# A two-layer decoder trunk on one core: the SwiGLU down projection by seven block products for eight, with its weights' sums and low parts made by GpSimd

## What is computed

```python
def swiglu(x, w_gate, w_up, w_down):
    return (jax.nn.silu(x @ w_gate) * (x @ w_up)) @ w_down
...
    f = swiglu(rms_norm(h, ffn_pre_g[i]), w_ff_gate[i], w_ff_up[i], w_ff_down[i])
    h = h + rms_norm(f, ffn_post_g[i])
    gate = jax.nn.sigmoid(rms_norm(h, ple_norm_g[i]) @ w_ple_gate[i])
    h = h + (p[i] @ w_ple_proj[i]) * gate
```

## Time and profile before

| what | value |
|---|---|
| median of 3 runs | 2053.27 us (2048.46 to 2055.60) |
| the profiled execution's own time | 2056.85 us |
| its span, first to last instruction | 2055.1 us |
| its mean granted TensorE clock | 0.987 of full |
| PE, DVE, ACT, POOL busy | 96%, 65%, 37%, 8% of the span |

### The profile page before, as it was taken

One profiled execution on the slowest core, in us unless ns is written; L12 is line 12 of the kernel. 1 busy time (PEld: TensorE's weight loads), 2 busy tenths in 40 slices (PEclk: granted clock), 3 DMA queues, 4 the chain that ended last, 5 costly groups with the idle time before them and its releaser, 6 DMA issues.

```text
span 2055.1 us, 27329 instructions
## 1 busy us (share of the span) xinstructions
PE 1983.0 (96%) x9412; PEld 1631.3 (79%) x9412; DVE 1330.7 (65%) x2126; ACT 750.5 (37%) x1402; POOL 161.1 (8%) x218
## 2 busy tenths in 40 slices
PE   6789999999999999999999997999999999999999
PEld 6668888888888878888866686788888888888887
DVE  5885666666566667477578657666566666655763
ACT  4552222333222243343268644333222233322431
POOL 2200000000000011110036311000000000000110
PEclk8999999999999999999999998999999999999999
DMA  5232222233232251231000112233232223323402
GB/s 187 99 106 93 89 79 87 77 102 97 82 92 78 86 194 37 67 108 52 0 11 2 52 52 97 82 103 97 82 92 77 86 77 102 97 82 106 170 11 82
DMA packets 214756, 173.25 MB, mean 84 GB/s; under 512 B 8608, under 2 KB 196384, under 8 KB 214688
## 3 DMA queue, kind: packets, MB, share of 16 engines
q1 hardware_dynamic: 212960, 166.08, 25.6%
q10 hardware_dynamic: 1728, 6.29, 0.9%
HBM read 159.75 MB, written 12.58 MB: 84 GB/s over the span
## 4 chain that ended last, share of the span: by engine, by line
PE 89%; DVE 6%; POOL 2%; issue 1%; DMA 1%; ACT 1%; SPq 0%; DVEq 0%; ACTq 0%
PE ps L285 15%; PE ps L287 15%; PE ps L286 15%; PE ps L690 13%; PE ps L692 13%; PE ps L691 13%; POOL probs L1352 1%; PE ps L346 1%; DVE ps L1317 1%; PE ps L1306 1%; PE ps L1360 1%; PE ps L563 1%; DVE t_lo L933 1%; PE ps L467 1%; DMA H<-in_x 0%
## 5 line engine op out<-in xcount | busy, mean ns | idle before, releaser
L1008 DVE TENSOR_TENSOR H<-H,ps 128x512 f32<-128x512 f32 x320 | 218.0, 685 | 142.2 <-PE ps L287 142.2
L285 PE MATMUL ps<-wd_hi,ffn_a_hi 128*128 128x512 f32 x704 | 275.1, 391 | 2.4 <-DVE H L1008 1.8
L287 PE MATMUL ps<-wd_hi,ffn_a_lo 128*128 128x512 f32 x704 | 274.6, 390 | 0.0
L286 PE MATMUL ps<-wd_lo,ffn_a_hi 128*128 128x512 f32 x704 | 274.5, 390 | 0.0
L690 PE MATMUL ps<-t_hi,s_hi 128*128 128x512 f32 x528 | 207.7, 393 | 16.8 <-DVE t_lo L933 16.1
L691 PE MATMUL ps<-t_lo,s_hi 128*128 128x512 f32 x528 | 207.0, 392 | 0.0
L692 PE MATMUL ps<-t_hi,s_lo 128*128 128x512 f32 x528 | 206.9, 392 | 0.0
L776 ACT ACTIVATE s_hi<-s_raw 128x512 fp32r<-128x512 f32 x176 | 111.1, 633 | 228.3 <-DVE s_raw L896 225.0
L896 DVE TENSOR_TENSOR s_raw<-s_raw,a_raw 128x512 f32<-128x512 f32 x88 | 60.8, 691 | 191.1 <-DMA s_raw<-in_w_ff_gate 143.6
L800 ACT ACTIVATE m<-ps 128x512 f32<-128x512 f32 x44 | 25.9, 589 | 405.0 <-PE ps L692 405.0
L285 PEld LDWEIGHTS ps<-wd_hi,ffn_a_hi 128*128 128x128 f32 x704 | 132.6, 188 | 31.4 <-issue 4.0
(11 more groups left out here) (208 smaller groups left out, 4183.3 us busy)
## 6 DMA issues: line engine op xcount, KB each, us to landing
a_raw<-in_w_ff_gate SPq DMA_DIRECT2D x88, 256.0 KB, 2.9
a_raw<-in_w_ff_up SPq DMA_DIRECT2D x88, 256.0 KB, 3.0
s_raw<-in_w_ff_up SPq DMA_DIRECT2D x88, 256.0 KB, 2.9
s_raw<-in_w_ff_gate SPq DMA_DIRECT2D x88, 256.0 KB, 3.0
wd_raw<-in_w_ff_down SPq DMA_DIRECT2D x44, 512.0 KB, 4.2
residual_spill<-H SPq DMA_DIRECT2D x16, 512.0 KB, 2.6
raw<-in_w_ple_gate SPq DMA_DIRECT2D x16, 512.0 KB, 5.7
back<-residual_spill SPq DMA_DIRECT2D x16, 512.0 KB, 6.9
```

What stands on the lines that cost most here:

```text
L285: pe.matmul(out_, lhs[0], rhs[0], start=first, stop=False)
L286: pe.matmul(out_, lhs[0], rhs[1], start=False, stop=False)
L287: return pe.matmul(out_, lhs[1], rhs[0], start=False, stop=last)
L1008: dve.tensor_tensor(dst, dst, ps[:, 4 + n % 4, :], ALU.add).then_inc(F["summed"][n % 4], 1)
```

## The change

The down projection of a group is done by the same scheme of seven for eight. Its tokens are taken in two halves (h = 0, 1) of 512; in each, a block is two token tiles (j = 0, 1) by one channel tile, and the weights' blocks are channel tile by column half. That is 7 blocks by 2 token tiles by 3 matmuls = 42 matmuls a half, 84 a group. A half now needs: four sums of activation blocks (`d_sums`, DVE, 128x256), their high and low parts (`d_his` ACT, `d_los` DVE), four bank copies (ACT) and 12 additions to H (`d_adds`, DVE) where there were 8. The two halves are not run after the group: they stand inside the next group's first tile, h = 0 after S3 and h = 1 after S1. In the layer's last group they stand at the end with nothing beside them.

The sums of weight blocks (gate, up and down) move from DVE to Pool, and so do the low parts of the seven down weight blocks, in four batches (three of 128x1024, one of 128x512). The sigmoid and DVE's product become one Silu on ACT. S2's sum is written into A21's slot; S3's low part lies over S3's raw block, which S2's sum reads, so `form_lo` of S3 now waits for S2's sum. Loads are put in a new order; the region of SBUF grows by 2 KB a partition. Cut to its core (`d_sums`, `d_his` and the copies left out):

```diff
+        DOWN = (("S3", 0, 7), ("A11", 0, 4), ("A11", 1, 3), ("S3", 1, 6), ("A12", 0, 4), ("S2", 0, 5), ("A12", 1, 3),
+                ("S2", 1, 7), ("S1", 0, 5), ("A22", 0, 6), ("S1", 1, 7), ("S4", 0, 5), ("A22", 1, 3), ("S4", 1, 7))
...
+        def ffn_load_down(sp, L, g):
+            sp.wait_ge(F["down"], PRODUCTS * (half_of(L, g, 0) + 1))
...
+        def ffn_load_tile(sp, L, g, t):
+            if not is_first(g, t):
+                ffn_load_after(sp, "S4", "a12", L, g, t, preceding(g, t))
+            if not is_last(g, t):
+                n = following(g, t)
+                ffn_load_after(sp, "A11", "a11", L, *n, (g, t))
+                sp.wait_ge(F["form_sum"], nth_sum("S4", L, g, t))
+                ffn_load(sp, "A21", "a21", L, *n)
+                for name, source in (("S3", "a11"), ("S2", "a22"), ("A12", "a12"), ("S1", "a22")):
+                    ffn_load_after(sp, name, source, L, *n, (g, t))
+            if t == 0 and not is_first(g, t):
+                ffn_load_down(sp, L, g)
+            if not is_last(g, t):
+                ffn_load_after(sp, "A22", "a22", L, *n, (g, t))
...
+        def ffn_pe_tile(pe, L, g, t):
...
             ffn_product(pe, "S3", L, g, t)
+            if t == 0:
+                ffn_pe_down(pe, L, g - 1, 0, (g, t))
...
             ffn_product(pe, "S1", L, g, t)
+            if t == 0:
+                ffn_pe_down(pe, L, g - 1, 1, (g, t))
             ffn_product(pe, "A22", L, g, t)
...
+        def ffn_act_second(act, L, g):
+            t, p, n = 1, (g, 0), following(g, 1)
+            gate_silu(act, L, *p, 1)
+            copy_first(act, L, g, t)
+            form_hi(act, "A22", L, g, t)
+            form_hi(act, "S4", L, g, t)
+            copy_m7(act, L, g, t)
+            wd_his(act, L, g, (0, 1))
+            copy_u(act, L, g, t)
+            wd_his(act, L, g, (2, 3))
+            if not is_last(g, t):
+                form_hi(act, "A11", L, *n)
+            gate_silu(act, L, g, t, 0)
...
+        def wd_los(pool, L, g):
+            r = GROUPS * L + g
+            pool.wait_ge(F["wd_sum"], 4 * r + 4)
+            for b in range(4):
+                slots = slice(2 * b, min(2 * b + 2, 7))
+                pool.wait_ge(F["wd_hi"], 4 * r + b + 1)
+                pool.tensor_tensor(wd_lo[:, slots, :], wd_raw[:, slots, :], wd_hi[:, slots, :].bitcast(F32), ALU.subtract
+                                   ).then_inc(F["wd"], 1)
...
+        def ffn_pool(pool, L, g):
+            n1, n2 = (g, 1), (g + 1, 0)
+            if not is_first(g, 0):
+                form_sum(pool, "S4", L, g, 0)
+            for name in ("S3", "S1", "S2"):
+                form_sum(pool, name, L, *n1)
+            wd_sums(pool, L, g)
+            form_sum(pool, "S4", L, *n1)
+            if not is_last(*n1):
+                form_sum(pool, "S3", L, *n2)
+            wd_los(pool, L, g)
+            if not is_last(*n1):
+                for name in ("S1", "S2"):
+                    form_sum(pool, name, L, *n2)
...
         def form_lo(dve, name, L, g, t):
             dve.wait_ge(F["form_hi"], nth(name, L, g, t))
+            if name == "S3":
+                dve.wait_ge(F["form_sum"], nth_sum("S2", L, g, t))
...
+        def ffn_dve_tile(dve, L, g, first_group=False):
+            t, p, n, down = 0, preceding(g, 0), following(g, 0), g - 1
+            times_up(dve, L, *p, 1)
+            form_lo(dve, "S2", L, g, t)
+            d_los(dve, L, down, 0)
...
+            d_adds(dve, L, down, 0, first_group)
+            form_lo(dve, "A12", L, g, t)
+            d_sums(dve, L, down, 1)
+            form_lo(dve, "S1", L, g, t)
+            d_los(dve, L, down, 1)
+            form_lo(dve, "A22", L, g, t)
+            form_lo(dve, "S4", L, g, t)
+            d_adds(dve, L, down, 1, first_group)
+            up_second_half(dve, L, g, t)
+            form_lo(dve, "A11", L, *n)
+            form_lo(dve, "S3", L, *n)
+            up_first_half(dve, L, g, t)
+            times_up(dve, L, g, t, 0)
+            form_lo(dve, "S2", L, *n)
+
+        def ffn_dve_second(dve, L, g):
+            t, p, n = 1, (g, 0), following(g, 1)
+            times_up(dve, L, *p, 1)
+            for name in ("A12", "S1", "A22", "S4"):
+                form_lo(dve, name, L, g, t)
+            if not is_last(g, t):
+                form_lo(dve, "A11", L, *n)
+            up_second_half(dve, L, g, t)
+            up_first_half(dve, L, g, t)
+            times_up(dve, L, g, t, 0)
+            d_sums(dve, L, g, 0)
+            if not is_last(g, t):
+                form_lo(dve, "S3", L, *n)
...
+                times_up(dve, L, last, 1, 1)
+                d_los(dve, L, last, 0)
+                d_adds(dve, L, last, 0)
+                d_sums(dve, L, last, 1)
+                d_los(dve, L, last, 1)
+                ffn_post(dve, L, 0)
+                d_adds(dve, L, last, 1, between=between)
```

More of the change, by code:

```diff
@@ L594, in trunk @@
              "S4": xb["b22"]}
[L595 to L599, removed]
+        W_RAW = {n: Z[f"{n.lower()}_raw"] for n in ORDER + ("A21",)}
+        m7, act_late = Z["m7"], ACT_LATE
@@ new lines, in trunk, with d_copy_first, d_copy_u @@
+        D_COPIED = (("A12", 0), ("A12", 1), ("S1", 0), ("S1", 1))
+        def d_copy_first(act, L, g, h, j):
+            u = half_of(L, g, h)
+            act.wait_ge(F["down"], nth_down("A11", j, u))
+            if j == 1:
+                act.wait_ge(F["summed"], nth_add(1, u))
+            act.activation(ps[:, (5, 7)[j], :], ps[:, (4, 3)[j], :], ACT.Copy).then_inc(F["d_copied"], 1)
+        def d_copy_u(act, L, g, h, j):
+            u = half_of(L, g, h)
+            act.wait_ge(F["down"], nth_down("S2", j, u))
+            act.wait_ge(F["summed"], nth_add((3, 5)[j], u))
+            act.activation(ps[:, (6, 3)[j], :], ps[:, (5, 7)[j], :], ACT.Copy).then_inc(F["d_copied"], 1)
@@ L856, in ffn_act_rest, with ffn_act_tile @@
             n = following(g, t)
+            for name in ("A11", "S3", "S2", "A12", "S1"):
+                form_hi(act, name, L, *n)
+        def ffn_act_tile(act, L, g):
+            t, p, n, down = 0, preceding(g, 0), following(g, 0), g - 1
+            gate_silu(act, L, *p, 1)
+            form_hi(act, "S2", L, g, t)
+            d_his(act, L, down, 0)
+            copy_first(act, L, g, t)
+            copy_m7(act, L, g, t)
+            form_hi(act, "A12", L, g, t)
+            for j in range(2):
+                d_copy_first(act, L, down, 0, j)
+            form_hi(act, "S1", L, g, t)
+            for j in range(2):
+                d_copy_u(act, L, down, 0, j)
+            form_hi(act, "A22", L, g, t)
+            form_hi(act, "S4", L, g, t)
+            copy_u(act, L, g, t)
+            d_his(act, L, down, 1)
+            form_hi(act, "A11", L, *n)
+            for j in range(2):
+                d_copy_first(act, L, down, 1, j)
+            form_hi(act, "S3", L, *n)
+            for j in range(2):
+                d_copy_u(act, L, down, 1, j)
+            gate_silu(act, L, g, t, 0)
+            for name in ("S2", "A12", "S1"):
+                form_hi(act, name, L, *n)
@@ new lines, in d_adds @@
+        def d_adds(dve, L, g, h, first_group=False, between=None):
+            u, bank_of, begun = half_of(L, g, h), {x[:2]: x[2] for x in DOWN}, set()
+            for k, (name, j, q, c) in enumerate(ADDS):
+                dve.wait_ge(F["down"], nth_down(name, j, u))
+                n = 4 * h + 2 * q + j
+                dst, src = H[:, n * D + c * HALF:n * D + (c + 1) * HALF], ps[:, bank_of[name, j], :]
+                if first_group and (n, c) not in begun:
+                    begun.add((n, c))
+                    dve.tensor_copy(dst, src).then_inc(F["summed"], 1)
+                else:
+                    dve.tensor_tensor(dst, dst, src, ALU.add).then_inc(F["summed"], 1)
+                if between:
+                    between(k)
@@ L1493, in ffn_loads @@
                 ffn_load(sp, "A12", "a12", L, *first)
+                if L == 1:
+                    sp.wait_ge(F["form_sum"], nth_sum("S4", 0, GROUPS - 1, 1))
+                ffn_load(sp, "A21", "a21", L, *first)
                 for j in range(5):
@@ L1497, in ffn_loads @@
                     sp.wait_ge(s["lo"][0], s.done("lo", PAIRS - 1))
-                ffn_load(sp, "A21", "a21", L, *first)
                 ffn_load(sp, "S2", "a22", L, *first)
@@ L1582, in _ @@
                 pool.sem_inc(s, 1)
+            pool.sem_inc(F["down"], PRODUCTS)
+            pool.sem_inc(F["summed"], SUMMED)
             pool.memset(minus_half, -0.5).then_inc(consts_set, 1)
```

571 lines of the change are left out of this document (291 added, 280 removed).

## The result

The changed kernel took 2137.0 us (median of 4 runs, 2136.2 to 2139.6) against 2053.9 us for the kernel before beside it (4 runs, 2048.5 to 2055.6): ratio 1.041, 95% interval [1.039, 1.043], 83 us slower. The forecast was 2083 us with a range of 2015 to 2115. Its sign was right, its size was not, and the result lies above the range.

What follows compares the result with a forecast made beforehand. The prediction took TensorE's matmuls as the bound (busy 96%), unless a new chain became longer. It summed 2056.85 - 59.8 (matmuls) + 60 (chain) + 19 (clock) + 11 (layer ends) = 2087, 2083 us against the median; range 2015 to 2115.

Steps and rivals of the forecast that it cites:

- Matmuls, 59.8 us less: TensorE: 84 down matmuls a group for 96, 12 x 22 groups x 0.2267 us; a group becomes 57.1 us.
- The down halves at nothing: Additions and bank copies of the down halves keep pace with TensorE (0.60 for 0.68 us), costed at nothing.
- Pool's prices: Pool's 128x512 operation taken at 1.2 us, between 1.18 and 1.28; skill estimate some 1.1 us.
- The chain: Pool's queue through S2's sum makes S3's low part late: TensorE waits 3.0 us in 20 group passages, 60 us.
- time 0: TensorE's start on A11 in a group's first tile, from which the chain's times are counted.
- two in three at 1.4 us: Clock falls behind two in three of 20 waits, losing 1.4 us each: 19 us, bounds 0 and 28.
- Start and end of a layer: Start 0, give or take 2 us; uncovered halves at the end 5.5 us a layer, 11 us, bounds 0 to 18.
- its uncovered chain: Chain to S3's low part if no Pool and DVE operations met: ends at 59.4, 0.4 us before its time.
- its second rival: Gain and wait cancel: wait of 2.2 to 2.8 us at full clock, 2047 to 2059 us; chance 0.09.
- the kernel in which the chain fits: Rival: Pool's S2 sum in time, TensorE waits 0 to 1.5 us, 2005 to 2035 us; chance 0.32.

Runs made afterwards that it cites:

- the version without the listed wait: Changed kernel with the down weights' low parts made by VectorE after its four low parts in the second tile, not by Pool: 2029.02 us, ratio 0.987; repeat 2026.24 us.
- the unused matmuls: Changed kernel with 12 more matmuls, results unused, between A11 and S3 of every group's first tile: 2097.05 us, ratio 1.020.
- the run whose waits were 1.0 to 1.8 us: Changed kernel with S1's and S2's sums after Pool's second low part and S3's low part ahead of VectorE's short sums: 2122.57 us, ratio 1.034.

## Why the forecast was right or wrong

- **Matmuls, 59.8 us less: right.** In the version without the listed wait a group takes 57.65 us for 59.85, against the 57.1 that were computed. The half microsecond between is the end of the same chain, 0.2 us late, and a slower start behind it.
- **The down halves at nothing: right.** In the middle of a layer no addition, copy or low part of theirs made TensorE wait.
- **Pool's prices: the upper bound was true.** A sum of 128x512 alone took 1.28 to 1.30 us, not 1.2. The estimate of 1.1 us from the Trainium skill (GPSIMD Engine Reference, 3.1 Elementwise) would have been further off. The forecast had 1.28 at hand, as the upper of its two prices.
- **The chain: right in each link, short by half a microsecond.** By time 0 of 279.0: Pool's start at 36.6 (forecast 37.2), S4's sum done at 44.9 (44.8), S3's from 48.7 to 50.0 (48.35 to 49.55), S2's done at 62.0 (61.3), S3's low part ready at 63.3 (62.8). The wait was 3.5 us as listed, 3.7 from where S3 was due, and not 3.0: 71 us (74) for 60. The term mis-sized is in the main Pool's 1.2 us a sum, with five sums ahead of the low parts and two behind.
- **Clock, "two in three at 1.4 us": this step failed.** All twenty waits were followed by the fall, and each cost 2.0 us by the unused matmuls, 2.3 by the timelines: 40 to 45 us for 19, outside the term's own bounds of 0 to 28. The forecast read one window of 3 us behind each wait in the earlier trace rows and took its loss of 1.4 us for the whole. By the timeline the two waits cost 1.7 us each, and in the changed kernel nine of the twenty passages lost 2.9. It also counted a wait of 3.30 us without a fall as one chance in three. Its window (90 to 94) ends where that wait ends, so it could not show the matmuls behind; the 3 us behind stand at 1.00 too. In the changed kernel the wait at the same place was 3.69 us, and the fall did follow it. So the reading was true, but nothing to take odds from.
- **Start and end of a layer, "5.5 us a layer": this step failed too.** The two waits that it named came as drawn (2.11 and 3.19 us for 2.3 and 3.1). What it set at nothing is the rest, in layer 0 3.4 us more of slow matmuls than before and 2.7 us of waiting for H. It cost 12 us in layer 0 and 14 in layer 1, 26 us for 11, where the bound was 18. Why the end is that long stays open (see above). The start of a layer was at zero as forecast (first S3 at 110.4 in both).

By the measured terms the sum is 2056.85 - 59.8 + 74 + 45 + 26 = 2142 us for 2136.15 measured; some 4 us of the difference were regained between the layers and 2 in the SwiGLU, where the kernel before has short waits of its own. The forecast had 2087: the clock makes 26 of the 55 us between the two sums, the ends 15, the wait 14. Two small slips of the forecast change nothing: its uncovered chain adds up to 59.3 and not 59.4, and its second rival to 2049 to 2061 and not 2047 to 2059.

The rivals: the kernel in which the chain fits is the one with the low parts on VectorE, and its 2026 to 2029 us lie in the 2005 to 2035 of that rival. Half of these instructions, or an earlier S2 sum, did not bring it about. Within the forecast the order of causes was right; the range ended at 2115, and two terms (clock and ends) went past their own upper bounds. They are not independent: the clock falls behind the same waits that make up the other terms, and behind part of those at the layer's end.

## What to carry to other kernels

An offload from VectorE to Pool is no gain in engine time if both read two inputs from SBUF: they take turns, so price the work at Pool's duration (9.3 us here for 5.2), as time in which VectorE's own two-input work stands still, and compare it with VectorE's real idle time before moving it. Price a new wait of TensorE as the wait plus the slow matmuls behind it, measured over the whole low stretch (3.5 + 2.0 us here). Matmuls of no use in the gap give the second part back, and in the run whose waits were 1.0 to 1.8 us there was no second part. Keep the schedule and move only the low parts: 2026 to 2029 us, 1.3% faster than the kernel before and 5% faster than the changed one. Whether the sums too would be better on VectorE was not tried.

## What the hardware showed that was not expected

- The fall of the clock followed each of the twenty waits of 3.5 us, and none of the forty of 1.0 to 1.8 us in the run with the late short sums. Between them the length alone did not decide. In the changed kernel a wait of 2.11 us was followed by it at the end of layer 0 (779.77) and not at the end of layer 1 (1981.35), and with the wait of 2.70 us it was the other way round (811.24 and 2011.38). The 1.82 and 1.90 us of the earlier trace rows were both followed by it. Filled with twelve matmuls whose sum is never read, the gap of 3.5 us kept 2.4 GHz.
- Taking turns stretches short instructions most: a subtraction of 128x256, 0.42 us alone, took 2.60 us beside Pool's low part of 2.56 us.
- Two low parts on each of Pool and VectorE at once took 6.13 and 4.69 us for 4.7 and 1.9 alone: hardly anything was done side by side.
